# Two transformer blocks in one kernel: fill steps regrouped, rotation and masks moved to the vector engine, a projection block and a kept row placed anew

## What is computed

```python
# first block: projections, then gated delta rule (8 heads, chunks) and retention (4 heads)
lower = where(strict, einsum(k_beta, k) * decay, 0)
t_inv = triangular_solve(lower, eye)              # unit lower triangle
def step(state, ...):
    v_new = uu - ww @ state
    o = qe @ state + aqk @ v_new
    state = state * ld + kd.T @ v_new
qb, kb = rotary(qb, positions), rotary(kb, positions)   # t1*cos - t2*sin, t1*sin + t2*cos
ob = chunk_retention(qb, kb, vb)
# out projection, MLP; second block: projections, neighbourhood attention
scores = where(in_win, scores + bias, NEG_INF); p = softmax(scores)
# grouped-query and memory attention, merge, 16 experts that each choose 64 tokens
ye = (silu(xs @ w_g) * (xs @ w_u)) @ w_down * gate
y = zeros.at[idx].add(ye)
x = layer_norm(ALPHA * x + y)
```

## Time and profile before

| | |
|---|---|
| median of three runs | 2493.96 us (2492.32 to 2495.08) |
| the profiled execution | 2495.81 us |
| its span | 2493.4 us |
| granted clock of PE, mean | 0.993 |
| PE busy | 97% of the span |
| DVE, ACT, POOL busy | 45%, 34%, 7% |
| memory traffic | 160 GB/s over the span |

### The profile page before, as it was taken

How to read it: one execution, slowest core, us unless ns; L and a number is a source line. 1 busy time by engine, 2 the same in 40 slices (tenths; PEclk the granted TensorE clock), 3 DMA queues, 4 the chain that set the end, 5 groups by cost and what they waited for, 6 DMA issues and landing times.

```text
span 2493.4 us, 31478 instructions
## 1 busy us (share of the span) xinstructions
PE 2409.8 (97%) x13446; PEld 1801.1 (72%) x13446; DVE 1123.6 (45%) x1527; ACT 840.2 (34%) x1339; POOL 168.6 (7%) x156
## 2 busy tenths in 40 slices
PE   8999999999999999999999999998999979999997
PEld 6787788887887888878888887865788834444442
DVE  6747575536434424344344463568433731112213
ACT  7444535234333323233333343447422211000001
POOL 0203020212101000000000001210000000000000
PEclk9999999999999999999999999999999989999999
DMA  5112213132323324232222243231322579999996
GB/s 166 68 53 84 93 44 110 52 119 81 105 85 118 118 102 169 102 135 102 102 93 82 96 153 127 81 135 48 118 87 66 202 323 406 428 427 427 427 428 270
DMA packets 117098, 400.97 MB, mean 161 GB/s; under 512 B 6368, under 2 KB 24416, under 8 KB 104032
## 3 DMA queue, kind: packets, MB, share of 16 engines
q1 hardware_dynamic: 112800, 384.28, 40.1%
q0 software_dynamic: 4160, 14.68, 1.7%
HBM read 385.06 MB, written 13.89 MB: 160 GB/s over the span
## 4 chain that ended last, share of the span: by engine, by line
PE 82%; DVE 9%; DMA 5%; ACT 3%; issue 2%; SPq 0%; DVEq 0%; POOL 0%; ACTq 0%; POOLq 0%
PE banks L94 19%; PE banks L96 19%; PE banks L95 19%; PE banks L2212 7%; PE banks L2250 5%; PE banks L2167 2%; DMA activations_T<-w_gate_up_in 1%; DMA ring<-w_gate_up_in 1%; PE banks L1641 1%; DVE ring_split L88 1%; DMA work<-o_b 1%; PE banks L1647 1%; DMA ring<-w_up_in 1%; DVE const L2814 1%; DVE work_split L88 1%
## 5 line engine op out<-in xcount | busy, mean ns | idle before, releaser
L94 PE MATMUL banks<-work_split,ring_split 128*128 128x512 f32 (+1 forms) x1560 | 620.9, 398 | 2.4 <-issue 0.8
L88 DVE TENSOR_TENSOR ring_split<-ring,halves_split 128x1024 fp32r<-128x1024 f32 x281 | 354.5, 1271 | 579.4 <-ACT halves_split L83 579.0
L95 PE MATMUL banks<-work_split,halves_split 128*128 128x512 f32 x1512 | 589.7, 390 | 0.0
L96 PE MATMUL banks<-activations_T_split,halves_split 128*128 128x512 f32 x1160 | 452.9, 390 | 0.0
L83 ACT ACTIVATE halves_split<-ring 128x1024 fp32r<-128x1024 f32 x281 | 293.4, 1054 | 311.0 <-PE banks L96 237.2
L94 PEld LDWEIGHTS banks<-work_split,ring_split 128*128 128x128 f32 x1560 | 293.3, 188 | 70.6 <-issue 8.8
L95 PEld LDWEIGHTS banks<-work_split,halves_split 128*128 128x128 f32 x1512 | 284.3, 188 | 56.4 <-issue 1.2
L96 PE MATMUL banks<-ring_split,work_split 128*128 128x512 f32 (+1 forms) x736 | 283.6, 385 | 0.0
L95 PE MATMUL banks<-halves_split,work_split 128*128 128x512 f32 x672 | 261.9, 390 | 0.0
L96 PEld LDWEIGHTS banks<-activations_T_split,halves_split 128*128 128x128 f32 x1160 | 217.8, 188 | 46.3
L96 PEld LDWEIGHTS banks<-ring_split,work_split 128*128 128x128 f32 x736 | 138.2, 188 | 27.8
(11 more groups left out here) (362 smaller groups left out, 3233.8 us busy)
## 6 DMA issues: line engine op xcount, KB each, us to landing
ring<-w_in_in SPq DMA_DIRECT2D x31, 2048.0 KB, 7.8
work<-w_gate_up_in SPq DMA_DIRECT2D x29, 2048.0 KB, 22.0
ring<-w_gate_up_in SPq DMA_DIRECT2D x21, 2048.0 KB, 22.6
ring<-w_down_in SPq DMA_DIRECT2D x19, 2048.0 KB, 9.1
work<-w_down_in SPq DMA_DIRECT2D x11, 2048.0 KB, 22.7
ring<-w_in_in SPq DMA_DIRECT2D x17, 1024.0 KB, 7.7
ring<-w_up_in SPq DMA_DIRECT2D x8, 2048.0 KB, 7.7
activations_T<-w_gate_up_in SPq DMA_DIRECT2D x8, 2048.0 KB, 21.6
```

Of the source, the lines that this page charges most:

```text
L88: s.mark(dve.tensor_tensor(R(dst), src, R(hi).bitcast(F32), ALU.subtract), what)
L94: pe.matmul(out, R(ll), R(rh), start=start, stop=False)
L95: pe.matmul(out, R(lh), R(rh), start=False, stop=False)
L96: return pe.matmul(out, R(lh), R(rl), start=False, stop=stop)
```

## The change

Five edits. The fill table has all six fill steps of a level between P and Y/X, and all four of a state step between V and S/O; DVE evacuates Y of both heads before X of both. The keys' rotation moves from POOL to DVE behind the queries', and head 0's results go to `PT_hi`, which needs no store to have ended. The third block of the second projection gets a buffer of its own, `wx`, and is loaded behind x3 (with its readers, and the wait of ACT's split, changed to match); block 4 then waits for block 0's last group. Masks 2 and 3 are added on DVE, behind steps 6 and 10 of the attention. The third `kept` matmul of the last pair moves behind its rows.

```diff
@@ -29,7 +29,7 @@
-FILL = dict(root=8, scores=6, turn=6, inverse=4, level=(3, 3), w=4, state=(2, 2), out=16)
+FILL = dict(root=8, scores=6, turn=6, inverse=4, level=(6, 0), w=4, state=(4, 0), out=16)
@@ -171,7 +171,7 @@
             (2, 512), (1024,), (NT, 512), (NT, 512), (NT, 512), (4, 512), (512,), (2, 512), (2, 512)])
-        qkT_hi = PT_hi
+        qkT_hi = qkT_0 = PT_hi
         ring_b = [ring[2], ring[1], ring[0]]
@@ -204,6 +204,7 @@
         (hx,), _ = carve(work, A1 + 6400, [(4, 512)])
+        (wx,), _ = carve(work, A0 + 4096, [(KB, 512)])
         (mgT, y_n, y_n_hi, sg2, mtmp), _ = carve(work, A0, [(KB, 512), (4, 512), (4, 512), (4, 512), (2, 512)])
...
@@ -572,10 +577,12 @@
                 q = n % 2
-                sp.wait_ge(*(d_pe(("p11.1", "m3.1")[q]) if n < 2 else p_pe(f"g{last_group[n - 2]}")))
-                w2[q].mark(sp.dma_start(ring[q][:, :, 0:width], src[:, :, col:col + width]), f"w{n}")
+                if n != 2:
+                    sp.wait_ge(*(d_pe(("p11.1", "m3.1")[q]) if n < 2 else p_pe(f"g{last_group[0 if n == 4 else n - 2]}")))
+                    w2[q].mark(sp.dma_start(slot2(n)[:, :, 0:width], src[:, :, col:col + width]), f"w{n}")
                 if n == 1:
                     sp.wait_ge(*d_vec("x3"))
+                    w2[2].mark(sp.dma_start(wx, order[2][0][:, :, order[2][1]:order[2][1] + 512]), "w2")
                     n2_tab.mark(sp.dma_start(const[:, rope_at:rope_at + 256], T["rope_g"]), "rope")
@@ -755,30 +762,10 @@
-            def rope_k(h):
-                if h == 0:
-                    pool.wait_ge(*b_tab("decay"))
-                    for j in range(2):
-                        pool.wait_ge(*oa_st[j]("o.3"))
-                    pool.wait_ge(*g_act(f"e{b_group(3)}"))
-                else:
...
-                b_pool.mark(i, f"ropek.{h}")
...
-            rope_k(0)
             for h in range(1, B_HEADS):
-                rope_k(h)
                 store_b(h - 1)
@@ -827,8 +814,6 @@
                 store_y("n", b)
-                if b < 2:
-                    add_mask(b + 2)
...
@@ -2222,7 +2207,7 @@
                         pe.wait_ge(*e_vec(f"SGT.{p}"))
-                        for t in range(3):
+                        for t in range(2):
                             kept(0, t)
@@ -2250,7 +2235,9 @@
                     return mm
-                if not last:
+                if last:
+                    kept(0, 2)
+                else:
                     gather(p + 1, range(4))
@@ -2436,11 +2423,11 @@
                         c_vec.mark(i, f"Y{s}_{j}.{p}")
-                        if s < LEVELS - 1:
...
+                    for j in range(2) if s < LEVELS - 1 else []:
+                        part = slice(0, HB) if s == LEVELS - 2 else slice(0, P)
+                        dve.wait_ge(*c_pe(f"X{s}_{j}.{p}"))
+                        dve.wait_ge(*c_vec(f"X{s - 1}_{j}.{p}"))
+                        c_vec.mark(dve.tensor_tensor(X[j][part, :, :], by_t(bank_b[j][part, 0:NT * HB]), X[j][part, :, :], ALU.add), f"X{s}_{j}.{p}")
                     fill(sum(FILL["level"]))
@@ -2477,22 +2464,27 @@
-            def rope_q(h):
+            def rope(h, what):
+                x, to = (0, 0) if what == "q" else (2, 2)
+                t, o4 = rk if h and what == "k" else rt, qkT if h else qkT_0
                 if h == 0:
-                    dve.wait_ge(*g_act(f"e{b_group(1)}"))
+                    dve.wait_ge(*g_act(f"e{b_group(x + 1)}"))
                     dve.wait_ge(*b_tab("decay"))
+                else:
+                    dve.wait_ge(*bg_act(f"e{x + 1}.{h}"))
+                    dve.wait_ge(*b_pe(f"S3.{h - 1}"))
+                if h == 1 and what == "k":
                     for j in range(2):
                         dve.wait_ge(*oa_st[j]("o.3"))
-                else:
-                    dve.wait_ge(*bg_act(f"e1.{h}"))
-                    dve.wait_ge(*b_pe(f"S3.{h - 1}"))
                 for o, (c0, c1, op) in enumerate(((cosT, sinT, ALU.subtract), (sinT, cosT, ALU.add))):
-                    dve.tensor_tensor(rt[:, 0, :], qkr[:, 0, :], c0, ALU.mult)
-                    b_rope.link(dve, dve.tensor_tensor(rt[:, 1, :], qkr[:, 1, :], c1, ALU.mult))
-                    i = dve.tensor_tensor(qkT[:, o, :], rt[:, 0, :], rt[:, 1, :], op)
+                    dve.tensor_tensor(t[:, 0, :], qkr[:, x, :], c0, ALU.mult)
+                    b_rope.link(dve, dve.tensor_tensor(t[:, 1, :], qkr[:, x + 1, :], c1, ALU.mult))
+                    i = dve.tensor_tensor(o4[:, to + o, :], t[:, 0, :], t[:, 1, :], op)
                     if o == 0:
                         b_rope.link(dve, i)
-                b_rope.mark(i, f"ropeq.{h}")
+                b_rope.mark(i, f"rope{what}.{h}")
+                if h == 0 and what == "q":
+                    dve.wait_ge(*b_rope("ropeq.0"))
@@ -2553,7 +2545,8 @@
                     split_b(h, n)
-                rope_q(h)
+                rope(h, "q")
+                rope(h, "k")
                 gate_b(h - 1)
@@ -2563,7 +2556,8 @@
                 out_b(h - 1)
-            rope_q(0)
+            rope(0, "q")
+            rope(0, "k")
             for h in range(1, B_HEADS):
@@ -2807,7 +2801,7 @@
                         if u == 0:
-                            dve.wait_ge(*bias_pool(f"bias{B}"))
+                            dve.wait_ge(*(bias_pool(f"bias{B}") if B < 2 else vec(f"mask{B}")))
                         vec.mark(dve.tensor_tensor(sc[:, i % 2, :, :], src, bias[B % 2][:, :, (0, 1, 1, 2)[u], :], ALU.add), f"s{i}")
@@ -2819,6 +2813,10 @@
                     vec.mark(dve.tensor_tensor(p, p, pinv[:, c:c + 2].unsqueeze(2).broadcast_to([P, 2, nk]), ALU.mult), f"n{m}")
+                if fam == "a" and i in (6, 10):
+                    b = (i + 2) // 4
+                    dve.wait_ge(*bias_ld[b % 2](f"bias{b}"))
+                    vec.mark(dve.tensor_tensor(bias[b % 2], bias[b % 2], bmask.unsqueeze(1).broadcast_to([P, 2, 3, 256]), ALU.add), f"mask{b}")
                 m, per = (i - 4, 2) if fam == "m" else (i - 3, 4)
```

More of the change, by code:

```diff
@@ L284, in build @@
         bg_pe, bg_act = sig("b_gemm_pe"), sig("b_gemm_act")
-        b_pe, b_act, b_vec, b_pool = sig("b_attn_pe"), sig("b_attn_act"), sig("b_attn_vec"), sig("b_attn_pool")
+        b_pe, b_act, b_vec = sig("b_attn_pe"), sig("b_attn_act"), sig("b_attn_vec")
         x_back, o_row, f_row = sig("x_again", 16), sig("mix_row", 16), sig("ff_row", 16)
@@ L354, in piece2, with slot2 @@
                 width = 256 if n == 5 else 512
-                return ring[n % 2][:, 2 * q:2 * q + 2, 0:width], row_hi(n, q)
-            return ring[n % 2][:, :, q * P:(q + 1) * P], h_col[q]
+                return slot2(n)[:, 2 * q:2 * q + 2, 0:width], row_hi(n, q)
+            return slot2(n)[:, :, q * P:(q + 1) * P], h_col[q]
+        def slot2(n):
+            return wx if n == 2 else ring[n % 2]
         def attn_of(fam, i):
@@ L1034, in evacuate_b @@
                     act.wait_ge(*b_rope(f"ropeq.{h - 1}"))
-                    act.wait_ge(*b_pool(f"ropek.{h - 1}"))
+                    act.wait_ge(*b_rope(f"ropek.{h - 1}"))
                     bg_act.mark(act.activation(qkr[:, g, :], psum[g % 2][:, :], ACT.Copy), f"e{g}.{h}")
@@ L1064, in high_qk @@
                 high(act, b_act, qkT_hi[:, 0:2, :], qkT[:, 0:2, :], f"qk0.{h}")
-                act.wait_ge(*b_pool(f"ropek.{h}"))
+                act.wait_ge(*b_rope(f"ropek.{h}"))
                 high(act, b_act, qkT_hi[:, 2:4, :], qkT[:, 2:4, :], f"qk1.{h}")
@@ L1266, in split2 @@
                 if p % 4 == 0:
-                    act.wait_ge(*w2[p // 4 % 2](f"w{p // 4}"))
+                    act.wait_ge(*w2[2 if p == 8 else p // 4 % 2](f"w{p // 4}"))
                 w, hi = piece2(p)
@@ L1732, in scores_b @@
                 pe.wait_ge(*b_rope(f"ropeq.{h}"))
-                pe.wait_ge(*b_pool(f"ropek.{h}"))
+                pe.wait_ge(*b_rope(f"ropek.{h}"))
                 pe.wait_ge(*(b_vec(f"oT3.{h - 1}") if h else c_vec("oT11.3")))
@@ L1742, in scores_b @@
                         else:
[L1743 removed]
+                            mm = pe.matmul(psum[2 + m][:, m * P:], qkT_0[:, 2 + k, m * P:(m + 1) * P], qkT_0[:, k, m * P:],
                                            start=(k == 0), stop=(k == 1))
@@ L1962, in project @@
                             lhs = [v[:, k, at * P:(at + 1) * P] for v in (x_hi, x)]
-                            rhs = (row_hi(n, k // 2)[:, k % 2, 0:N], ring[slot][:, k, 0:N])
+                            rhs = (row_hi(n, k // 2)[:, k % 2, 0:N], slot2(n)[:, k, 0:N])
                         else:
@@ L2438, in chain_a @@
                         c_vec.mark(i, f"Y{s}_{j}.{p}")
-                        if s < LEVELS - 1:
-                            part = slice(0, HB) if s == LEVELS - 2 else slice(0, P)
-                            dve.wait_ge(*c_pe(f"X{s}_{j}.{p}"))
-                            dve.wait_ge(*c_vec(f"X{s - 1}_{j}.{p}"))
```

(3 more changed lines are left out.)

9 lines of the change are left out of this document (removed).

## The result

| | before | changed |
|---|---|---|
| median | 2494.52 us (2492.32 to 2497.01, 4 runs) | 2480.03 us (2477.57 to 2481.30, 4 runs) |
| profiled execution, its span | 2495.81, 2493.4 | 2479.27, 2477.4 |
| PE, DVE, POOL busy | 97%, 45%, 7% | 97%, 45%, 5% |

The ratio of the two kernels is estimated at 0.9935, with a 95% interval of 0.9923 to 0.9946: 13.5 to 19.2 us faster. (The quotient of the two medians, 0.9942, lies inside it.) The forecast was 2478.6 us.

The account below looks back on a forecast made before the run. PE was taken as the bound, busy 2409.8 of 2493.4 us. Terms -10.3 - 3.0 - 2.4 + 0.3 + 0 = -15.4 took 2495.81 to 2480.4; less 1.85 to the median, 2478.6 us, range 2471 to 2488.

Parts of the forecast that it names:

- Stage A: New fill table in stage A: passages -7.2, waits for ACT -5.9, new waits +2.8, together -10.3 us.
- The passage: Levels of stage A: going from projection matmuls to small tiles and back costs 0.36 us; 20 fewer give -7.2 us.
- The states: State steps of stage A: full 128x128 tiles lose no passage, so regrouping 16 steps saves 0.
- The waits for ACT: Stage A: PE's waits for ACT's evacuations, 3.4 us in levels and 2.5 in state steps, vanish under longer fill: -5.9 us.
- The new waits: Stage A: PE waits for DVE at three kinds of late place, 1.0, 0.9 and 0.9 us, together +2.8.
- The rival of DVE's late evacuations: Stage A: DVE's group-end work delays evacuations at 21 group ends, +31.5 us instead of +2.8; 2507.3 us, slower, chance 0.05.
- Rotation: Retention, rotation moved from POOL to DVE: head 0 -2.2 us, later heads' splits -0.8, together -3.0.
- Third block: Second projection: own buffer and earlier load remove PE's wait behind ACT's split, -2.4 us, bounds -2.6 and -1.6.
- Kept row: Last experts: the moved row only lengthens a wait for weights and falls into a DVE wait: 0, bounds -0.95 and +0.3.
- Masks: Attention, two mask additions moved from POOL to DVE: net +0.3 us, between -2.9 and +4.
- then come the copy of a finished product and step 7: Attention, DVE after the first mask ends at 1678.0: 0.6 + 2.2 us, to 1680.8 against 1680.15 before, +0.6.
- The sign that I had named: Attention, new profile: DVE idle for a table before the first mask, and some 3 us wait for the normalising operation remaining.

## Why the prediction was right, point by point

**Stage A** held, nearly term by term. The passage: 0.36 forecast, 0.37 in the timeline (7.62 to 7.25) and 0.38 with one step put back. The states: free, as the earlier trace rows had it. The waits for ACT: gone, and back at 2.5 with the old state fill. The new waits: 2.8 forecast, 2.4 measured in the three places named. The rival of DVE's late evacuations was right about the place and wrong about the size; DVE's new order, which I had not priced, kept 1.75 us of it away. The measured terms, -7.4 for the passages, -5.9 and +2.4, make -10.9, where the stretch gave -10.0. The 0.9 is spread. Some 0.3 lies in the state steps, where the old fill brought back 1.6 while the waits changed by 1.9. The rest is in the levels, where a start can be later than its wait says, as in the rotation below: level 2 of the rounds with convolutions takes 7.93 to 7.94 from P to P, 0.7 over the 7.25, where a wait of 0.47 is all that shows in two of them.

**Rotation** came out at -3.6 for -3.0. Head 0's gain I put down to two things, the dropped wait for the store and 12 operations at 0.69 in place of 1.7; the run that waits for the store again has the same time, so the second is enough by itself and the first was not needed. By the run with the later keys on POOL, head 0 gave 2.2, as forecast, and the later heads 1.4 for 0.8. The second is a reading error: I took the wait of 0.41 at 608.39 as the loss. A matmul is shown 0.39 long where the next is due after 0.23, so a wait counts from too late an end. The one ahead starts at 607.59, and 0.80 to the next start, 0.23 of it due, is 0.57; the start behind it comes 0.31 later instead of 0.23. (Timeline of PE, kernel before:)

```profile
607.59 0.39 PE L96 MATMUL banks<-ring_split,work_split 128*128 128x512 f32 x1
608.39 0.47 PE L94 MATMUL banks<-halves_split,activations_T_split 128*128 128x512 f32 x1 [0.41 <-DVE work_split L88]
608.70 0.39 PE L95 MATMUL banks<-halves_split,work_split 128*128 128x512 f32 x1
```

Twice 0.65 is 1.3 of the 1.4.

**Third block** as forecast, -2.3 for -2.4. **Kept row** as forecast, 0, and in the way described.

**Masks** were the term that was mis-sized, +0.3 against +1.2 in the profiled execution. The step "then come the copy of a finished product and step 7" looked at the wrong customer: PE waited 2.54 us for that copy itself, at the products that reuse its bank, before step 7 mattered. I had seen that wait and given it no price. The sign that I had named, a wait of some 3 us for the normalising operation, is not there. Behind the wait for the copy the clock was down for some 3 us, 0.6 to 0.9 us more, which no sum of waits contains. Without that fall the move costs 0.3 to 0.4, which is the forecast's size by another wait than the forecast's.

The sum was -15.4, and the medians gave -14.5. The stretches with a forecast add up to -10.0 - 3.6 - 2.3 + 1.2 + 0 = -14.7. The two misses, -0.6 in the rotation and +0.9 in the masks, mostly cancel, and that they do is luck.

## What to carry to other kernels

Where independent fill stands between the links of a dependent chain, put it in one place per link, on the side where the slow engine's answer is awaited: it saves a change of tile shape per link and doubles the cover. But look at what then stands without cover on the other side, and put the evacuation that is wanted first ahead on that engine. Before an operation with a wait is moved onto an in-order engine, find out when its input lands and move the load first: the same masks cost up to 1.2 us or gained 3.5, with the table late or there.

## What the runs showed of the hardware

A short pause of TensorE can cost more than itself. A gap of 3.16 us was followed by 2.7 us at a granted clock of 0.50, the lower of the two levels, and six matmuls 0.43 apart instead of 0.23; behind the gap of 2.58 at the same place before, the clock stayed at 1.00. After waits of 2.2 to 2.6 in the attention it fell in five profiles and stayed up in three, and with waits of the same length the stretch differed by 0.6 to 0.9 us. With the masks on POOL it fell behind a wait of 1.9 and not behind one of 2.0. So the length of the pause does not decide by itself.

What makes the profiles differ where the program is the same is the first 25 us (by up to 2.1 us), the router's stretch (by 2.0) and the attention (by 1), not the long stretches between. In the router's stretch and in the attention the difference goes with a fall of the clock behind a pause of 1.9 to 2.6 us.
